# Delta mixer: query, key and head norms kept as token columns, gates first, output slots begun chunk by chunk

## The chip, the cores and the metric

The kernel runs on one core of one Trainium2 chip. The metric is the device time of one execution in microseconds (us); less is better. The core has a matrix engine (PE, its weight loads shown as PEld), a vector engine (DVE), an activation engine (ACT), a general engine (POOL) and a queue engine (SP) that issues loads. PE writes into eight banks of PSUM (128 partitions x 512 fp32 each); DVE and ACT read PSUM, POOL works on SBUF alone. Engines run on their own and wait for one another by semaphores.

## The reference

The program is a two-layer block (adaptive norms, SwiGLU halves, a gated-delta mixer in layer 0 and a window attention in layer 1) followed by a second two-layer block. The change touches the gated-delta mixer and, in one loop order, the three other output projections. Of the mixer this is computed, for 512 tokens (256 context, 256 latent), 8 heads of 128, in both directions:

```python
def _l2_normalize(x):
    return (xf * lax.rsqrt(jnp.sum(xf * xf, axis=-1, keepdims=True) + EPS))
...
qkv, z, ab = jnp.split(h @ w_in, [qkv_w, qkv_w + z_w], axis=-1)
qkv = jax.nn.silu(_short_conv(qkv, conv_w))
g = -jnp.exp(a_log) * jax.nn.softplus(ab[:, :, :, 0] + dt_bias)
beta = jax.nn.sigmoid(ab[:, :, :, 1])
return _l2_normalize(q), _l2_normalize(k), v, z, g, beta
...
# chunkwise gated delta rule in both directions, o_t = S_t^T q_t / sqrt(dk)
...
y = _rms_norm(o_f + o_b, o_gain) * jax.nn.silu(z)
return y.reshape(y.shape[0], y.shape[1], -1) @ w_out
```

So there are three norms over a head's 128 features: of each query, of each key, and of each head's output.

## The kernel before, in words

Activations are kept feature-major: a chunk is 128 features x 512 tokens. Every fp32 weight product is made from two parts, so `product` (lines 618 to 622) issues three matmuls: high x high, low of one x high, high x low. A weight slot (up to 128 x 2048) is loaded by SP into a ring of four; `high` on ACT (line 1287) rounds it into `w_hi`, which has two buffers, and POOL (line 2418, four instructions of 128x512) leaves the low part in `ring_lo`. PE then runs the slot. `slots_used` counts slots that PE is through with, and starts the next `high`.

**The input projection** (`delta_in`). `dn_in` has 16 slots of 48 matmuls, 128x512 each; the first runs chunk by chunk of the activations as the norm before it delivers them. DVE takes the two banks of each of slots 0 to 11 through a 5-tap convolution (lines 2208 and 2212) and a gate with ACT's tanh (lines 1620 and 2221); slots 12 to 15 are the z gate (lines 2230 and 2234). `pr_free` counts banks that are free again. Then comes the slot `dn_ab` (96 matmuls that write 32 columns each: the gates' inputs). Only then ACT squares the 16 query and key chunks (line 1631), PE sums over the 128 features by a matmul with ones, whose result stands in every partition (line 772), ACT takes the root (line 1666), and DVE takes a reciprocal of 128x512 and multiplies (`heads_norm`, lines 2269 and 2271). The decay gates follow, a matmul with a triangle (line 777), and the core.

**The core** (`delta_core`) has 8 units U, each for 4 heads and one 128-token chunk in both directions s. In a unit, six levels n of a triangular inversion alternate PE (lines 842, 854, 857) and DVE (lines 2320, 2328); work of the next unit is put between the levels: decay rows at n = 1 (line 793), the values turned to token-major at n = 2 (line 803, copied by ACT at line 1697), key products at n = 4 (line 809). DVE adds the outputs of both directions into `h` (line 2338).

**The output.** After the last unit `heads_norm` does the same for the 8 output heads (squares, ones matmul at line 943, root, reciprocal, gain, product with z at line 2277). ACT and POOL prepare the weights of `dn_out` after that; DVE splits `h` into high and low (lines 1805 and 1807); PE runs 4 slots of 48 matmuls, bank by bank, and DVE adds each to `x` (line 1861). `project_out` is also used for `swa_out`, `mla_out0` and `mla_out1`.

The order on each engine is the order in which the code is written.

## Time and profile before

| | |
|---|---|
| median of 3 runs | 3388.6 us (3388.38 to 3397.56) |
| the profiled execution's own time | 3385.27 us |
| its span | 3383.4 us |
| PE busy | 3099.0 us (92%), 23172 matmuls |
| DVE / ACT / POOL busy | 43% / 34% / 46% |
| chain that ended last, by engine | PE 56%; POOL 19%; issue 15%; DVE 7%; ACT 2% |

The span is the first to the last instruction; the execution's own time is 1.9 us longer. A busy PE means that a matmul is in flight, not that PE is at its peak. PEclk is the clock that PE was granted, as a share of 2.4 GHz: 1.00 is 2.4 GHz, 0.50 is 1.2 GHz, and a stretch between has parts at both. In a timeline row the bracket tells how long the engine sat idle before the row and which instruction ended that; where there is no bracket the idle time was under about 0.15 us. "x48 3.07" rows are merged: so many instructions that follow one another, and the time from the first's start to the last's end.

### The profile page before, as it was taken

The page shows a single profiled execution, that of the slowest core. Times are in us where ns is not written, and L with a number is a line of the kernel's source. Part 1 is how long each engine was busy: PE and PEld are TensorE (multiplying, and loading weights), DVE is VectorE, ACT ScalarE, POOL GpSimd, SP SyncE. Part 2 cuts the span into 40 slices and gives each one's busy share as a digit, 9 for nine tenths or more (in the row PEclk, how much of TensorE's full clock was granted, in tenths as well). Part 3 has the DMA queues.
Part 4 walks back from the last instruction along what each step waited for, and adds up shares of the span by engine and source line. Part 5 has one row for each costly group of instructions (what it writes and reads, how often), then busy time and mean ns, then how long its engine had stood idle before and what let it go on. Part 6 is the DMA issues. An engine that isn't in the chain of part 4 may idle for free.

```text
span 3383.4 us, 56078 instructions
## 1 busy us (share of the span) xinstructions
PE 3099.0 (92%) x23172; PEld 2684.4 (79%) x23172; DVE 1454.7 (43%) x2565; ACT 1136.2 (34%) x1720; POOL 1540.5 (46%) x1183
## 2 busy tenths in 40 slices
PE   6999999949998489999899997989999899998998
PEld 4777778828887367777778877789987899887998
DVE  3222348585555732123321245542454452355452
ACT  2212223232222122121322224543354464454563
POOL 1444434301010334444344543179881588662686
PEclk8999989969999789999899998999999899999899
DMA  7534322200000133443433232045542355441454
GB/s 289 170 122 163 124 92 99 76 13 3 2 3 2 36 138 123 165 162 110 149 127 126 82 114 75 27 137 188 186 151 84 112 186 174 137 150 63 141 173 133
DMA packets 58915, 390.04 MB, mean 115 GB/s; under 512 B 6480, under 2 KB 7760, under 8 KB 21360
## 3 DMA queue, kind: packets, MB, share of 16 engines
q1 hardware_dynamic: 49472, 322.07, 27.7%
q10 hardware_dynamic: 9072, 64.25, 5.5%
q8 instruction: 132, 2.16, 0.3%
q0 software_dynamic: 192, 1.18, 0.1%
q14 instruction: 47, 0.39, 0.0%
HBM read 386.42 MB, written 1.05 MB: 115 GB/s over the span
## 4 chain that ended last, share of the span: by engine, by line
PE 56%; POOL 19%; issue 15%; DVE 7%; ACT 2%; DMA 0%; POOLq 0%; ACTq 0%; DVEq 0%
POOL ring_lo L2418 19%; PE bank L620 14%; PE bank L621 13%; PE bank L622 13%; DVE core L2269 2%; PE bank L655 1%; PE bank L1130 1%; PE bank L854 1%; PE bank L842 1%; PE bank L857 1%; DVE core L2328 1%; PE bank L1035 1%; PE bank L1141 1%; PE bank L793 1%; PE bank L1023 1%
## 5 line engine op out<-in xcount | busy, mean ns | idle before, releaser
L2418 POOL TENSOR_TENSOR ring_lo<-ring,w_hi 128x512 fp32r<-128x512 f32 (+1 forms) x833 | 1098.2, 1349 | 1301.6 <-ACT w_hi L1287 1301.3
L622 PE MATMUL bank<-h_hi,ring_lo 128*128 128x256 f32 (+1 forms) x3376 | 1117.8, 331 | 0.0
L620 PE MATMUL bank<-h_hi,w_hi 128*128 128x512 f32 (+1 forms) x2448 | 868.7, 355 | 100.1 <-POOL ring_lo L2418 70.6
L621 PE MATMUL bank<-h_lo,w_hi 128*128 128x512 f32 (+1 forms) x2448 | 854.3, 349 | 0.0
L622 PEld LDWEIGHTS bank<-h_hi,ring_lo 128*128 128x128 f32 x3376 | 654.3, 194 | 58.7
L620 PEld LDWEIGHTS bank<-h_hi,w_hi 128*128 128x128 f32 x2448 | 473.7, 194 | 181.3 <-POOL ring_lo L2418 65.0
L1287 ACT ACTIVATE w_hi<-ring 128x2048 fp32r<-128x2048 f32 (+2 forms) x227 | 395.6, 1743 | 439.9 <-PE bank L622 332.9
L621 PEld LDWEIGHTS bank<-h_lo,w_hi 128*128 128x128 f32 x2448 | 474.2, 194 | 53.6
L622 PE MATMUL bank<-hid_r,ring_lo 128*128 128x256 f32 (+1 forms) x1088 | 364.3, 335 | 0.0
L1877 DVE SCALAR_TENSOR_TENSOR core<-core,bank 128x512 f32<-128x512 f32 (+1 forms) x88 | 54.7, 621 | 641.8 <-ACT core L1355 641.8
L620 PE MATMUL bank<-hid_r,w_hi 128*128 128x512 f32 (+1 forms) x808 | 289.8, 359 | 2.3 <-POOL ring_lo L2418 2.3
L621 PE MATMUL bank<-hid_r,w_hi 128*128 128x512 f32 (+1 forms) x808 | 285.4, 353 | 0.0
L2418 POOL TENSOR_TENSOR ring_lo<-ring,h_hi 128x512 fp32r<-128x512 f32 (+2 forms) x156 | 199.0, 1305 | 103.4 <-ACT h_hi L1287 103.3
L622 PEld LDWEIGHTS bank<-hid_r,ring_lo 128*128 128x128 f32 x1088 | 206.6, 190 | 21.7
L2418 POOL TENSOR_TENSOR ring_lo<-ring,x_r 128x512 fp32r<-128x512 f32 (+2 forms) x156 | 199.9, 1312 | 43.5 <-ACT x_r L1287 43.3
L1355 ACT ACTIVATE core<-bank 128x512 f32<-128x512 f32 (+1 forms) x88 | 47.9, 545 | 492.8 <-PE bank L622 492.8
L1861 DVE SCALAR_TENSOR_TENSOR x<-bank,hgate,x 128x256 f32<-128x256 f32 x112 | 49.8, 480 | 323.1 <-PE bank L622 323.1
L2434 POOL TENSOR_TENSOR core<-core,con 128x512 f32<-128x512 f32 x16 | 20.3, 1287 | 347.0 <-DVE core L2304 347.0
L620 PEld LDWEIGHTS bank<-hid_r,w_hi 128*128 128x128 f32 x808 | 152.9, 189 | 30.9 <-issue 8.2
L621 PEld LDWEIGHTS bank<-hid_r,w_hi 128*128 128x128 f32 x808 | 153.0, 189 | 19.6
L620 PE MATMUL bank<-h_hi 128*128 128x256 f32 x464 | 136.3, 294 | 11.5 <-POOL ring_lo L2418 4.8
L620 PE MATMUL bank<-h_hi,x_r 128*128 128x256 f32 x464 | 131.9, 284 | 3.2 <-POOL ring_lo L2418 1.9
(373 smaller groups left out, 4737.5 us busy)
## 6 DMA issues: line engine op xcount, KB each, us to landing
ring<-w SPq DMA_DIRECT2D x88, 1024.0 KB, 4.9
zbuf<-ada_later ACTq DMA_DIRECT2D x60, 1024.0 KB, 4.9
ring<-up SPq DMA_DIRECT2D x48, 1024.0 KB, 4.8
ring<-w SPq DMA_DIRECT2D x64, 704.0 KB, 4.0
...
```

Source lines behind the costliest of these rows:

```text
L620: pe.matmul(out, a[0], b[0], start=start, stop=False)
L621: pe.matmul(out, a[0], b[1], start=False, stop=False)
L622: return pe.matmul(out, a[1], b[0], start=False, stop=stop)
L655: mm = pe.matmul(out[32 * j:32 * j + 32, :], cond[:, c, :], w[:, c * 256:(c + 1) * 256], start=(c < 4), stop=(c >= 4))
L793: mm = pe.matmul(dbank[s][A0][:, hd, :], dcol(TOK_G, U, s, hd).broadcast_to([P, P]), incl(s), start=True, stop=True)
L842: mm = pe.matmul(small4(s, C0)[r, hd, :], q[f"LT{U % 2}"][r, hd, r], identc[r, :] if n == 0 else q["X"][r, hd, :], start=True, stop=True)
L1287: ins = act.activation(part, like(ring[:, r, a:b], part), ACT.Copy)
L1355: act.activation(tanh2[:, u % 2, t0:T], psum[u % 2][:, t0:T], ACT.Tanh, scale=0.5).then_inc(tanh_done, 1)
L1861: ins = dve.scalar_tensor_tensor(xs, psum[OUT_BANK + c % 2][:, s * CTX:(s + 1) * CTX], gate[:, 2 * c + s:2 * c + s + 1], xs, ALU.mult, ALU ...
L1877: turn(dve.scalar_tensor_tensor(swu2[:, u % 2, t0:T], tanh2[:, u % 2, t0:T], 1.0, psum[u % 2][:, t0:T], ALU.add, ALU.mult))
L2269: step(dve.reciprocal(grec[:, c % 4, :], dstd[:, c % 8, :]))
L2418: ins = pool.tensor_tensor(like(ring_lo[:, r, a:b], part), like(ring[:, r, a:b], part), part.bitcast(F32), ALU.subtract)
```

## The change

The three norms are no longer applied to 128x512 tiles; the sums are formed as columns with one value per token, and the factors are moved to where a per-token factor is applied anyway. Queries and keys stay unnormalised in `qkv`. The key's inverse norm squared goes into beta (`norm_columns`), and the inverse norm itself into the copy of the values (`key_norm_col`). The query's norm scales only the output head, so it cancels in the head's norm but for the epsilon, which gets the query's sum (`query_eps`). The head's norm is summed per unit, and its root and reciprocal are taken once as 128x32; PE spreads the result over partitions by a matmul with the identity.

`dn_ab` is loaded and multiplied before the other slots of `dn_in` (within its first), with the 32 gate columns as stationary side and 512 tokens moving; four small matmuls turn it. The gates are made between slots 1 and 7. Squares and sums of queries and keys follow the slots one by one. The product with z moves to POOL, inside the core. In `project_out` the first slot of the four output projections runs chunk by chunk over both banks. `dn_in` is a plain unrolled loop on PE, ACT and DVE. Line numbers of the changed kernel differ: lines 620 to 622 before are 637 to 639 after.

```diff
-        STREAMS += [("dn_in", 16, 2048), ("dn_ab", 1, 256), ("dn_out", 4, 2048)]
+        STREAMS += [("dn_ab", 1, 256), ("dn_in", 16, 2048), ("dn_out", 4, 2048)]
...
-                    for q in range(2 if parts == 1 else 1):
+                    qs = range(2 if parts == 1 else 1)
+                    first = parts == 1 and n == 0
...
+                wab = weights(pe, "dn_ab", 0, 0)
+                for n in range(16):
...
+                        if n == 0 and q == 0:
+                            ab = product(psum[MISC][0:32, :], cut(wab, lambda v: v(c * 32, (c + 1) * 32)),
+                                         cut(hs, lambda v: v[:, c, :]), c == 0, c == DC - 1)
+                            if c == DC - 1:
+                                ab.then_inc(slots_used, 1)
...
-                over_slots(pe, 16, slot)
-
-                w = weights(pe, "dn_ab", 0, 0)
-                for tc in range(4):
-                    for c in range(DC):
-                        mm = product(psum[MISC][:, tc * 32:(tc + 1) * 32], cut(hs, lambda v: v[:, c, tc * CK:(tc + 1) * CK]),
-                                     cut(w, lambda v: v(c * 32, (c + 1) * 32)), c == 0, c == DC - 1)
-                mm.then_inc(slots_used, 1)
-
-                for c in range(16):
-                    pe.wait_ge(hs_done, c + 1)
-                    if c >= 2:
-                        pe.wait_ge(hstd_done, c - 1)
-                    pe.matmul(psum[4 + c % 2][:, :], ones, sqh[:, c % 4, :], start=True, stop=True).then_inc(hsum_done, 1)
-
-                pe.wait_ge(gates_done, 1)
-                pe.wait_ge(consts_in, 32)
-                for s in range(2):
-                    mm = pe.matmul(psum[MISC][:, 32 * s:32 * (s + 1)], incl(s), tokv(TOK_G)[:, 32 * s:32 * (s + 1)],
-                                   start=True, stop=True)
-                mm.then_inc(gate_pe, 1)
+                    if n == 1:
+                        pe.wait_ge(gate_act, 1)
+                        for tc in range(4):
+                            mm = pe.matmul(psum[STAT][:, 32 * tc:32 * tc + 32], ab_t[:, tc * P:(tc + 1) * P], ident[0:32, 0:32],
+                                           start=True, stop=True)
+                        mm.then_inc(gate_pe, 1)
+                    if 2 <= n < 10:
+                        for c in (2 * n - 4, 2 * n - 3):
+                            pe.wait_ge(hs_done, c + 1)
+                            for tc in range(4):
+                                j = 32 * (c // DNH) + tc * DNH + c % DNH
+                                mm = pe.matmul(psum[OUT_BANK][:, j:j + 1], sqh[:, c % 4, tc * P:(tc + 1) * P], ones[:, 0:1],
+                                               start=True, stop=True)
+                            mm.then_inc(hsum_done, 1)
+                    if n == 6:
+                        pe.wait_ge(gates_done, 1)
+                        pe.wait_ge(consts_in, 32)
+                        for s in range(2):
+                            mm = pe.matmul(psum[STAT][:, 128 + 32 * s:160 + 32 * s], incl(s), tokv(TOK_G)[:, 32 * s:32 * (s + 1)],
+                                           start=True, stop=True)
+                        mm.then_inc(gate_pe, 1)
...
+                def head_sums(U, s):
+                    pe.wait_ge(hs_done, 16 + U - 1 + s + 1)
+                    if U + 2 < UNITS_D:
+                        pe.wait_ge(dn["v"][s], U + 3)
+                    else:
+                        pe.wait_ge(dn["qd"][s], UNITS_D)
+                    for hd in range(QUAD):
+                        mm = pe.matmul(dwide[s][A1][:, hd:hd + 1], quad[s]["LT1"][:, hd, :], ones[:, 0:1], start=True, stop=True)
+                    mm.then_inc(hsum_done, 1)
...
+                            elif n == 3 and U % 2 == 0 and U > 0:
+                                head_sums(U - 1, s)
...
             def delta_out(k):
-                for c in range(DNH):
-                    pe.wait_ge(hs_done, 16 + c + 1)
-                    if c >= 2:
-                        pe.wait_ge(hstd_done, 16 + c - 1)
-                    pe.matmul(psum[6 + c % 2][:, :], ones, sqh[:, c % 4, :], start=True, stop=True).then_inc(hsum_done, 1)
+                pe.wait_ge(hn_done, 9)
+                for hd in range(DNH):
+                    if hd >= 6:
+                        pe.wait_ge(y_in_done, hd - 5)
+                    for tc in range(4):
+                        mm = pe.matmul(psum[HEAD_BANKS[hd % 6]][:, tc * P:(tc + 1) * P],
+                                       head_r[:, tc * DNH + hd:tc * DNH + hd + 1].broadcast_to([P, P]), ident, start=True, stop=True)
+                    mm.then_inc(hd_spread, 1)
                 project_out("dn_out", X_BEFORE[1], hs, DC, 1, 0, ready="dn_out")
...
-                high("dn_in", 1, 0, 1)
-                stream("dn_in", "dn_ab", proj, ahead=2)
-
-                for c in range(16):
-                    if c >= 4:
-                        act.wait_ge(hsum_done, c - 3)
-                    if c == 0:
-                        act.wait_ge(pr_free, 4 + 32)
...
+                high("dn_in", 1, 0, 1, free=BASE["dn_ab"])
+                for n in range(16):
+                    if n + 2 < 16:
+                        high("dn_in", n + 2, (n + 2) // RING, (n + 2) % RING)
...
+                        act.activation(ab_t, psum[MISC][0:32, :], ACT.Copy).then_inc(gate_act, 1)
+                    proj(n, n // RING, n % RING)
+                    if 1 <= n < 9:
+                        for c in (2 * n - 2, 2 * n - 1):
+                            act.wait_ge(pr_free, 4 + c + 1)
+                            if c >= 4:
+                                act.wait_ge(hsum_done, c - 3)
+                            act.activation(sqh[:, c % 4, :], qkv[:, c, :], ACT.Square).then_inc(hs_done, 1)
...
+                    if n == 10:
+                        act.wait_ge(hsum_done, 16)
+                        act.activation(tokv(TOK_T2)[:, 0:32], psum[OUT_BANK][:, 32:64], ACT.Sqrt, bias=eps).then_inc(hstd_done, 1)
...
+                for s in range(2):
+                    head_squares(UNITS_D - 1, s)
+                high("dn_out", 0, 0, 0)
+                act.wait_ge(hn_done, 8)
+                act.activation(head_r, head_r, ACT.Sqrt).then_inc(hstd_done, 1)
                 act_steps[0] = mine.n
-                act.wait_ge(y_in_done, DNH)
-                high("dn_out", 0, 0, 0)
+                for hd in range(DNH):
+                    act.wait_ge(y_in_done, hd + 1)
+                    act.activation(h_hi[:, hd, :], h[:, hd, :], ACT.Copy).then_inc(hh_done, 1)
                 stream("dn_out", "w1_010")
...
+            def head_squares(U, s):
+                act.wait_ge(dn["outd"][s], U + 1)
+                act.activation(quad[s]["LT1"], out_block(h, U, s), ACT.Square).then_inc(hs_done, 1)
...
-                    act.activation(quad[s]["V"], dbank[s][A1], ACT.Copy).then_inc(dn["v"][s], 1)
+                    for hd in range(QUAD):
+                        ins = act.activation(quad[s]["V"][:, hd, :], dbank[s][A1][:, hd, :], ACT.Copy, scale=key_norm_col(U, s, hd))
+                    ins.then_inc(dn["v"][s], 1)
...
+                    if k == 1:
+                        high("dn_in", 0, 0, 0)
...
+                def norm_columns():
+                    dve.wait_ge(gate_act, 4)
+                    dve.tensor_copy(tokv(TOK_GC), psum[STAT][:, 128:192])
+                    dve.wait_ge(hstd_done, 1)
+                    step(dve.tensor_scalar(query_eps, psum[OUT_BANK][:, 0:32], EPS, EPS * P, ALU.add, ALU.mult))
+                    r, rr = tokv(TOK_T3)[:, 0:32], tokv(TOK_T3)[:, 32:64]
+                    step(dve.reciprocal(r, tokv(TOK_T2)[:, 0:32]))
+                    step(dve.tensor_tensor(rr, r, r, ALU.mult))
+                    both = tokv(TOK_BETA).rearrange("p (d c) -> p d c", d=2)
+                    step(dve.tensor_tensor(both, both, rr.unsqueeze(1).broadcast_to([P, 2, 32]), ALU.mult))
+                    dve.tensor_scalar(tokv(TOK_NEGB), tokv(TOK_BETA), -1.0, None, ALU.mult).then_inc(gates_done, 1)
+
+                after = {1: gate_inputs, 4: decay_rate, 11: norm_columns}
...
-                heads_norm(16, DNH)
-                for c in range(DC):
-                    dve.wait_ge(y_in_done, c + 1)
-                    split("dn_out", c, h[:, c, :], 0)
+
+                dve.wait_ge(hstd_done, 2)
+                dve.reciprocal(head_r, head_r).then_inc(hn_done, 1)
+
+                def head_scaled(hd):
+                    dve.wait_ge(hd_spread, hd + 1)
+                    dve.scalar_tensor_tensor(h[:, hd, :], h[:, hd, :], p_("dn_gain"), psum[HEAD_BANKS[hd % 6]][:, :], ALU.mult, ALU.mult)\
+                        .then_inc(y_in_done, 1)
+
+                dve.wait_ge(hz_done, 8)
+                head_scaled(0)
+                head_scaled(1)
+                for hd in range(DNH):
+                    dve.wait_ge(hh_done, h_split("dn_out", hd))
+                    dve.tensor_tensor(h_lo[:, hd, :], h[:, hd, :], h_hi[:, hd, :].bitcast(F32), ALU.subtract).then_inc(hl_done, 1)
+                    if hd + 2 < DNH:
+                        head_scaled(hd + 2)
                 add_out("dn_out", k, 1, mod[:, k, 2, :], 0, squared=k + 1)
...
+                def head_mean(U, s):
+                    dve.wait_ge(hsum_done, 16 + U - 1 + s + 1)
+                    dve.scalar_tensor_tensor(head_cols(head_r, U, s), dwide[s][A1][:, 0:QUAD], 1.0 / P, head_cols(query_eps, U, s),
+                                             ALU.mult, ALU.add).then_inc(hn_done, 1)
...
+                def head_gate(U, s):
+                    pool.wait_ge(hs_done, 16 + U - 1 + s + 1)
+                    block = out_block(h, U, s)
+                    pool.tensor_tensor(block, block, out_block(zs, U, s), ALU.mult).then_inc(hz_done, 1)
```

How the instructions stand on PE where the projection ends and the core begins. Before: the last gate-input matmuls (128x32), 16 sums against ones (L772), two triangle matmuls (L777), and the core's first (L793, L803).

```order
L620 MATMUL bank<-w_hi,h_hi 128x32
L621 MATMUL bank<-ring_lo,h_hi 128x32
L622 MATMUL bank<-w_hi,h_lo 128x32
L772 MATMUL bank<-core,con 128x512 x16
L777 MATMUL bank<-tok,con 128x32 x2
L793 MATMUL bank<-con,tok 128x128 x8
L803 MATMUL bank<-con,big 128x128 x8
```

After: the last matmuls of slot 15 (L637 to L639) are followed by the core's first (L817 is L793 of before, L827 is L803).

```order
L637 MATMUL bank<-h_hi,w_hi 128x512
L638 MATMUL bank<-h_lo,w_hi 128x512
L639 MATMUL bank<-h_hi,ring_lo 128x512
L817 MATMUL bank<-con,tok 128x128 x8
L827 MATMUL bank<-con,big 128x128 x8
```

The 96 gate matmuls, the 16 sums and the 2 triangle matmuls no longer stand between slot 15 and the core. What takes their place stands between slots; this is PE at the end of slot 6 after the change (L794: one-column sums, L801: the triangle):

```order
L638 MATMUL bank<-h_lo,w_hi 128x512
L639 MATMUL bank<-h_hi,ring_lo 128x512
L794 MATMUL bank<-con,core 128x1 x8
L801 MATMUL bank<-tok,con 128x32 x2
L637 MATMUL bank<-h_hi,w_hi 128x512
```

Such eight one-column matmuls stand behind each of slots 2 to 9; before, two slots followed each other directly there.

DVE after the core's last outputs. Before, for each head a reciprocal, the gain and the product with z, and at the end the splits (L1805 and L1807, here the first two of the heads' last rows and the first of the splits):

```order
L2338 TENSOR_TENSOR h<-h,bank 128x4x128 x2
L2269 RECIPROCAL core<-core 128x512
L2274 SCALAR_TENSOR_TENSOR h<-h,par,core 128x512
L2277 TENSOR_TENSOR h<-h,zbuf 128x512
L2269 RECIPROCAL core<-core 128x512
```

After (L2404 is L2338 of before, L2364 the head means, L2327 gain and norm, L2335 the low part):

```order
L2404 TENSOR_TENSOR h<-h,bank 128x4x128 x2
L2364 SCALAR_TENSOR_TENSOR tok<-bank,tok 128x4 x2
L2323 RECIPROCAL tok<-tok 128x32
L2327 SCALAR_TENSOR_TENSOR h<-h,par,bank 128x512 x2
L2335 TENSOR_TENSOR h_lo<-h,h_hi 128x512
L2327 SCALAR_TENSOR_TENSOR h<-h,par,bank 128x512
```

Eight wide reciprocals became one of 32 columns, the product with z is gone from DVE, and the high parts are now ACT's.

## Rows read from the trace of the kernel before

**Rows 1.** Busy time by stretch, all engines; its columns are in its second line

```profile
core 0: us, PE busy (x) PEld busy (x) DVE busy (x) ACT busy (x) POOL busy (x), PEclk, DMA share, GB/s
600.00:660.00 60.00, 60.00 (x268) 49.71 (x266) 33.66 (x43) 14.56 (x16) 24.48 (x19) 1.00 0.21 72
660.00:677.00 17.00, 16.82 (x96) 16.72 (x95) 2.72 (x5) 1.31 (x3) 0.00 (x0) 0.61 0.19 63
677.00:746.60 69.60, 22.92 (x36) 6.88 (x36) 65.01 (x42) 25.34 (x41) 0.00 (x0) 0.62 0.04 15
746.60:1091.00 344.40, 312.65 (x6016) 295.60 (x6016) 183.92 (x442) 82.89 (x232) 35.53 (x28) 0.99 0.01 2
1091.00:1140.00 49.00, 8.65 (x16) 2.46 (x16) 45.04 (x33) 14.42 (x19) 5.37 (x4) 0.63 0.00 1
```

**Rows 2.** Instruction groups 677 to 745 us, DVE: busy us, mean ns, idle before

```profile
L2269 DVE RECIPROCAL core<-core 128x512 f32<-128x512 f32 x16 | 53.5, 3346 | 2.4 <-ACT core L1666 2.4
L2271 DVE SCALAR_TENSOR_TENSOR big<-big,core 128x512 f32<-128x512 f32 x16 | 11.1, 692 | 0.5
```

**Rows 3.** Timeline of PE: start us, us, instruction, idle before and what ended it

```profile
469.68 1.95 PE L639 MATMUL bank<-con,core 128*128 128x1 f32 x16 [1.70 <-DVE core L1817]
472.26 1.87 PE L647 MATMUL bank<-con,tok 128*128 128x128 f32 x8 [0.64 <-DVE tok L1828]
477.11 0.77 PE L620 MATMUL bank<-h_hi,w_hi 128*128 128x512 f32 x1 [2.97 <-DVE h_lo L1842]
482.78 0.40 PE L621 MATMUL bank<-h_lo,w_hi 128*128 128x512 f32 x1
493.59 0.79 PE L620 MATMUL bank<-h_hi,w_hi 128*128 128x512 f32 x1 [2.67 <-POOL ring_lo L2418]
```

**Rows 4.** Timeline of DVE and ACT, slots 1, 11 and 15 of dn_in

```profile
507.94 0.75 DVE L2208 TENSOR_SCALAR core<-bank,par 128x512 f32<-128x512 f32 x1 [6.25 <-PE bank L622]
616.74 0.75 DVE L2208 TENSOR_SCALAR core<-bank,par 128x512 f32<-128x512 f32 x1 [0.39 <-PE bank L622]
625.76 0.64 ACT L1620 ACTIVATE core<-core 128x512 f32<-128x512 f32 x1 [4.01 <-DVE core L2212]
...
660.02 1.29 DVE L2230 TENSOR_SCALAR core<-bank 128x512 f32<-128x512 f32 x2 [8.20 <-PE bank L622]
661.41 1.29 DVE L2234 SCALAR_TENSOR_TENSOR zbuf<-core 128x512 f32<-128x512 f32 x2
```

**Rows 5.** Chain that ended last, from 746 us: start us, us, what

```profile
746.65 3.75 PE bank L793 x16
```

**Rows 6.** Timeline inside one unit of the core

```profile
858.86 0.60 ACT L1697 ACTIVATE core<-bank 128x512 f32<-128x512 f32 x1 [0.30 <-PE bank L803]
862.15 0.63 PE L854 MATMUL bank<-core 64*64 64x64 f32 x16
```

**Rows 7.** Timeline from the core's last output to the second slot of dn_out

```profile
1090.35 0.69 DVE L2338 TENSOR_TENSOR h<-h,bank 128x512 f32<-128x512 f32 x1 [1.10 <-PE bank L893]
1092.30 1.28 ACT L1666 ACT_TABLE_LOAD   x1
...
1132.64 3.71 ACT L1287 ACTIVATE w_hi<-ring 128x2048 fp32r<-128x2048 f32 x2 [30.00 <-DVE h L2277]
1134.63 11.95 POOL L2418 TENSOR_TENSOR ring_lo<-ring,w_hi 128x512 fp32r<-128x512 f32 x8 [77.42 <-ACT w_hi L1287]
1136.21 1.63 DVE L1807 TENSOR_TENSOR h_lo<-h,h_hi 128x512 fp32r<-128x512 f32 x1
...
1147.49 0.69 DVE L1807 TENSOR_TENSOR h_lo<-h,h_hi 128x512 fp32r<-128x512 f32 x1
1155.74 0.88 DVE L1861 SCALAR_TENSOR_TENSOR x<-bank,mod,x 128x256 f32<-128x256 f32 x2 [6.49 <-PE bank L622]
1156.77 0.47 PE L620 MATMUL bank<-h_hi,w_hi 128*128 128x512 f32 x1 [1.06 <-DVE x L1861]
```

**Rows 8.** Timeline of PE, first slot of mla_out1

```profile
3118.59 0.38 PE L620 MATMUL bank<-h_hi,w_hi 128*128 128x256 f32 x1 [2.55 <-DVE h_lo L1807]
```

172 lines of the change are left out of this document (85 added, 87 removed).

## The prediction

> **What bounds the kernel now.** I read first the page's head (PE busy 92%), then busy time by stretch [rows 1], then the groups and timelines of the places that the change touches, PE's first. [Rows 1] name the bound of each stretch. From 600 to 660 us PE is busy all the time at clock 1.00: here matmul time counts. From 660 to 677 us PE does only the 96 gate-input matmuls, at clock 0.61, and DVE has 2.72 us of work. From 677 to 746.6 us DVE is busy 65.01 of 69.6 us and PE 22.9: DVE's reciprocals bound. From 746.6 to 1091 us, the core, PE is busy 312.65 of 344.4 us. From 1091 to 1140 us DVE is busy 45.04 of 49 us, PE 8.65. So the edits at the two stretches that DVE bounds can give time back, and edits in the two that PE bounds cost what they put on PE. The sum is made against the profiled execution's own time, 3385.3 us; it lies 3.3 us below the median of 3388.6, which is added back at the end. A measurement of this kernel can tell 0.3%, 10 us, from no change.
>
> **1. The start of dn_in.** Slot 0 is 48 matmuls. The first 13 take 477.11 to 482.78, 0.436 each; then the clock is up. When they are done PE waits 2.67 us for `ring_lo` (POOL), and slot 1 begins cold, 0.79 for its first matmul, as slot 0's was 0.77 [rows 3]. DVE takes a slot once both its banks are done: slot 1 at 507.94 and slot 15 at 660.02, 14 slots later [rows 4], so a warm slot lasts 10.863 us and a matmul 0.2263. Afterwards slot 0 has 72 matmuls, 24 of them for the gates: 482.78 + 59 x 0.2263 = 496.1. POOL is ready by then (at 493.59 before), so there is neither the wait nor a second cold start, and slot 1 ends at 496.1 + 10.9 = 507.0; with 0.2 for the semaphore DVE has it at 507.2. **Gain: 0.8 us**; the gate matmuls cost nothing, since they take the place of the wait (2.67) and the cold start (13 x 0.21 = 2.7). Were the wait still there, the cost would be 2 us. One change could bring it: the cast of slot 0's weights now waits until PE is through with the last slot of the product before, at 469.68 - 1.70 = 467.98 [rows 3]; the cast takes 1.9 (half of 3.71) and POOL's four pieces 4 x 11.95 / 8 = 6.0 [rows 7], so they end at 475.9, ahead of 477.11 where slot 0 starts.
>
> **2. Between the slots.** The sums of 16 chunks are 64 one-column matmuls. Sixteen of that kind took 1.95 us [rows 3], 0.122 each: 7.8 us. Four transposes and two triangle matmuls add 0.8 (eight 128x128 ones took 1.87 cold): 8.6. Bounds: 5, if they overlap their neighbours, and 15, if each takes the 0.234 of that 128x128 row. ACT's squares (16 x about 0.6, as its 0.64 for a 128x512 tanh) fit in the 4.01 us that it idles in front of a tanh, twice per slot. DVE is near its limit: in a slot of 10.86 us it waits 0.39 us for PE [rows 4]. Its gate work (12 to 14 instructions of 32 to 64 columns, some 3 us in all after slots 1, 4 and 11) goes into that slack, into the 1.0 us by which each slot with sums is longer, and into slots 12 to 15, where it has 2.6 of 10.86 us to do. ACT's table changes (1.28 each [rows 7], four or five) fall in its idle time too. So DVE's start in slot 15 is 660.02 - 0.8 + 8.6 = 667.8. It needs 2.7 us from there for the z gate (660.02 to 661.41 + 1.29), and with 0.1 for the semaphore the core starts at 670.6. Before it started at 746.65 [rows 5]. **Gain: 76.0 us.** What goes is the 17.0 us of gate matmuls and the 69.6 us of norms, in which 16 reciprocals took 53.5 and 16 multiplies 11.1 [rows 2]. What comes last next is the z gate: the core's first matmuls write banks that it reads.
>
> **3. The core.** Sums of a unit's heads stand behind level 3 of units 2, 4 and 6: 8 one-column matmuls, 1.0 us each time, and PE is what the chain goes through there: L854 of the next level would start that much later [rows 6]. **Cost: 3.0 us.** Costed at nothing: the copy of the values in 4 pieces instead of one of 0.60 (L1697; ACT is busy 83 of 344 us, and the values are wanted one unit later), six squares on ACT, six products with z on POOL, which is busy 36 of 344 us [rows 1], and six means of 4 columns on DVE. If ACT's cover is gone, 7 copies cost 1.1 us more each and 6 squares 0.6: that makes 14 the upper end, and 0 the lower (sums in PE's own gaps, of which it has 32 us).
>
> **4. From the core to dn_out.** Call T the end of the last output, 1090.35 + 0.69 = 1091.04 [rows 7]. After T: square 0.6 and a semaphore, 0.7; ACT casts slot 0's weights, 1.9 (3.71 for two), to 2.6; table load 1.28, to 3.9; a root of 32 columns 0.25 (my estimate, under the 0.64 of 512 columns [rows 4]), a reciprocal of 32 columns 0.21 (a sixteenth of 3.346 [rows 2]), and semaphores: the spreads start at T + 4.7. They are 32 matmuls of 128 columns: at 0.234 until the clock is up, then half: 6.8 us, so the first product is at T + 11.5. Slot 0 now runs chunk by chunk, 48 x 0.2263 = 10.9, to T + 22.4. It needs one head per 1.36 us; DVE gives one per 0.7 + 0.69 = 1.4 (the 0.69 is L1807's at 1147.49), and with a start two heads ahead isn't in the way. Slot 1's weights: ACT has the 8 high parts of `h` first, up to T + 17.6, then the cast, to 19.5, then POOL's four pieces at 11.95 / 8 = 1.5, to T + 25.2. So POOL, not PE, sets slot 1's start. Before it was 1156.77 = T + 65.7. That is 40.5 us earlier. The wait of 2.6 us ahead of it is like that of 2.67 in front of 493.59, behind which slot 1 of dn_in started cold; there 13 matmuls at 0.436 instead of 0.2263 cost 2.7. I take off 2.0. **Gain: 38.5 us.** Bounds: 26 (rival C) and 43 (no cold start, ACT's copies beside DVE).
>
> L1807 took 1.63 us at 1136.21, while POOL made low parts, and 0.69 at 1147.49, when it had ended [rows 7]. The Trainium skill, "GPSIMD Engine Reference", section "Key points", says that POOL shares its SBUF interfaces with VectorE and that DVE instructions with two SBUF inputs are among those that suffer. By it the low parts stretch and the scaling, whose second operand is in PSUM, does not. By the row alone all 16 may stretch by 0.94; that is 1.88 per head, rival C's price.
>
> **5. The other output projections.** In mla_out1 PE waits 2.55 us for the last chunk's low part while only its first bank's matmuls are there to do [rows 8]; mla_out0 has the same wait, 2.54, and swa_out has none. With both banks chunk by chunk PE has twice the work per chunk. **Gain: 4.8 us**, between 0 and 5.1.
>
> **Sum**: 76.0 - 3.0 + 38.5 + 4.8 = 116.3, profiled time 3269.0; with 3.3 added the median is 3272.
>
> **Rivals.**
> B, the squares couple the engines: each wait for ACT's squares in 8 slots costs PE another 1.3 us (two squares), 10.4, and the values' and squares' copies in the core take half of its upper end, 14 / 2 = 7 (3 are in the forecast): 3272 + 10.4 + 4 = 3286 to 3288. For it: DVE has only 0.39 us of slack per slot [rows 4], and squares wait for DVE's gate. Against it: sums lag their slot by one, and ACT idles 4.01 us.
> C, the tail is paced by DVE under POOL: POOL works on slots 0 and 1 while DVE scales and splits; with 1.88 more per head it gives the last head at T + 11.5 + 8 x 3.28 = 37.7, and slot 1 follows; 65.7 - 37.7 - 2 = 26 instead of 38.5: 3284. For it 1.63 against 0.69. Against it: slot 0's four POOL pieces end near T + 9, and slot 1's begin after T + 19.
> D, more than forecast: the one-column sums disappear beside their neighbours (up to 7.8 in dn_in, 3 in the core, of which I take two thirds) and dn_out has no second cold start (2): 3272 - 9 = 3263.
> E, slower: the inserted one-column matmuls bring the clock down to 1.2 GHz in slots 2 to 15. Then 14 x 48 matmuls take 0.436 instead of 0.2263: 141 us lost against 116 won, 3413. It decides from 11.5 slots on, 10.1 us each. For it: the stretch of 32-column matmuls had 0.61, busy 16.82 of 17.0 us. Against it: the core, of 6016 short matmuls with gaps, has 0.99 [rows 1].
> The Trainium skill, "TensorE: Matmul & The Clock Gate", section "HAM oscillation — how this bites in real kernels", reports kernels that lose clock to short idle gaps between groups of matmuls; by it alone the time would be E's, by the row of the core, with far more gaps at 0.99, the forecast's.
> F, it doesn't do what it says, and the core still waits for something of the old chain. On PE nothing but slot 15 now stands ahead of the core, and the last gate step on DVE comes after slot 11, so this is all but excluded.
>
> **Chances.** Forecast 0.60 (own range 3262 to 3282), B 0.17, C 0.13, D 0.07, E 0.02, F 0.01. Faster by over 0.3%: 0.97; within: 0.01; slower: 0.02. The range 3260 to 3292 takes in forecast, D, B and C and leaves out the combinations of B and C.
>
> **What would show it.** DVE's start in slot 15 near 667.8 and the core's first matmul near 670.6 (steps 1, 2); a slot with sums at 11.9 us instead of 10.86, at clock 1.00 (else B or E); a core of about 347 us instead of 344.4, with level 4 of units 2, 4 and 6 late by 1 us (step 3); the first product of dn_out at T + 11.5 and slot 1 at T + 25, with a wait for `ring_lo` ahead of it (step 4; with DVE's low parts at 1.6, C); no wait over 1 us for `h_lo` in mla_out0 and mla_out1 (step 5). The forecast is wrong above all if the core's start or dn_out's slot 1 is off by over 5 us.

## The result

| | before | after |
|---|---|---|
| median | 3391.99 us (4 runs, 3388.38 to 3397.56) | 3279.45 us (4 runs, 3276.90 to 3281.89) |
| ratio | | 0.967, 95% interval 0.9653 to 0.9688 |
| profiled execution | 3385.27 us, span 3383.4 | 3281.89 us, span 3280.1 |
| PE busy | 3099.0 us, 23172 rows | 3077.8 us, 23316 rows |

The median was forecast at 3272 and the profiled execution at 3269.0. The medians are 112.5 us apart, the two profiled executions only 103.4: the profiled execution of the kernel before lies 6.7 us below its median, that of the changed one 2.4 above. Single executions scatter more than the steps argued about here: the kernel before took 3382 to 3402 us in all runs of this study, the changed one 3272 to 3290. So the steps are judged by marks inside the profiles, that is, by the times at which named instructions start.

The stretches of the kernel after that answer to [rows 1]: slot 0 to slot 1 of dn_in, slots 1 to 15, the z gate, the core, and from the core to slot 1 of dn_out. The columns are those of [rows 1].

```profile
core 0: us, PE busy (x) PEld busy (x) DVE busy (x) ACT busy (x) POOL busy (x), PEclk, DMA share, GB/s
476.70:506.90 30.20, 30.20 (x121) 22.10 (x121) 19.12 (x39) 12.20 (x18) 10.07 (x8) 0.91 0.20 71
506.90:675.70 168.80, 168.78 (x813) 141.72 (x812) 111.14 (x158) 56.89 (x67) 67.42 (x52) 1.00 0.25 88
675.70:678.60 2.90, 0.05 (x1) 0.08 (x1) 2.72 (x5) 1.23 (x2) 0.00 (x0) 1.00 0.68 192
678.60:1026.70 348.10, 316.69 (x6072) 299.36 (x6072) 184.25 (x448) 94.31 (x287) 44.11 (x35) 1.00 0.01 4
1026.70:1052.50 25.80, 21.44 (x121) 19.05 (x122) 12.02 (x23) 11.74 (x14) 11.46 (x10) 0.87 0.00 1
```

The two stretches that DVE bounded are gone; PE is busy without a gap in all of dn_in. Mark by mark, profile against profile:

| step | forecast gain | measured | from |
|---|---|---|---|
| 1, slot 1 of dn_in | 0.8 | 0.5 | 507.94 to 506.97, less 0.45 by which dn_in began earlier |
| 2, core's start | 76.0 (with step 1) | 67.7 | 746.65 to 678.55, less the same 0.45 |
| 3, core | -3.0 | -3.8 | 344.4 to 348.2 |
| 4, slot 1 of dn_out | 38.5 | 39.9 | 65.7 to 25.8 behind the core |
| 5, mla_out0 and 1 | 4.8 | 5.1 | waits of 2.54 and 2.55 gone |
| not forecast | | 2.3 | dn_in's earlier start 0.45, rest of dn_out 1.1, later 0.8 |
| not forecast | | -1.5 | near 2120 us the clock is at 1.2 GHz for 6.8 us, before for 3.4 |
| not forecast | | -11.5 | one DVE copy of 12.35 us |
| not forecast | | 5.1 | given back in stages behind the copy |
| sum | 116.3 | 103.3 | |

### Slots 1 to 15

DVE's timeline, starts of slots 1, 2, 3 and 15 (answers to [rows 4]):

```profile
506.97 0.75 DVE L2256 TENSOR_SCALAR core<-bank,par 128x512 f32<-128x512 f32 x1 [1.52 <-PE bank L639]
519.08 0.75 DVE L2256 TENSOR_SCALAR core<-bank,par 128x512 f32<-128x512 f32 x1 [1.78 <-PE bank L639]
531.80 0.75 DVE L2256 TENSOR_SCALAR core<-bank,par 128x512 f32<-128x512 f32 x1 [3.43 <-PE bank L639]
...
675.72 1.29 DVE L2278 TENSOR_SCALAR core<-bank 128x512 f32<-128x512 f32 x2 [8.20 <-PE bank L639]
```

Slot 15 was forecast at 667.8. PE's instruction groups between 507 and 672 us say why (columns as in [rows 2]):

```profile
L794 PE MATMUL bank<-con,core 128*128 128x1 f32 x128 | 14.7, 245 | 0.0
L786 PE MATMUL bank<-con,core 32*128 32x32 f32 x8 | 1.1, 274 | 0.0
L801 PE MATMUL bank<-tok,con 128*128 128x32 f32 x4 | 0.6, 276 | 0.0
```

The program has 64 one-column matmuls, and the trace 128 rows of them, 14.7 us instead of 7.8. Transposes and triangle have twice their number too. A slot with sums takes 12.72 us, 1.84 more than one without (10.88), not 1.0. PE waits for nobody in these slots: the squares never come late (rival B), and the clock is 1.00 (rival E). Nor do the sums disappear beside their neighbours (rival D).

### The core

PE in unit 2, around the sums of unit 1's heads (answers to [rows 6]):

```profile
789.85 0.68 PE L878 MATMUL bank<-core 64*64 64x64 f32 x16
790.78 0.68 PE L878 MATMUL bank<-core 64*64 64x64 f32 x16 [0.25 <-DVE core L2394]
791.40 2.11 PE L843 MATMUL bank<-con,core 128*128 128x1 f32 x16
793.44 1.12 PE L890 MATMUL bank<-core 64*64 64x64 f32 x16
```

and granted clock around the same place (PE alone):

```profile
786.00:791.40 5.40, 5.15 (x113) 1.00 0.01 3
791.40:793.40 2.00, 2.00 (x20) 0.91 0.03 8
793.40:796.60 3.20, 3.20 (x63) 0.52 0.00 0
796.60:800.00 3.40, 3.07 (x57) 1.00 0.00 0
```

The sums are 16 rows, 1.95 to 2.1 us, all on the path. Behind them the clock is at 1.2 GHz for 3 us; that adds 1.5 us in unit 2. In units 4 and 6 it stays at 2.4 GHz. From each unit's decay rows to the next ones the loss is 3.5 us in unit 2 and 2.0 in unit 4. From those of unit 6 to the core's end it is 1.0, but here the two kernels do not compare as they stand. The kernel before loses clock 7.5 us before the end of its core, the changed one does not (first row before, second after):

```profile
1083.06 3.41 PE L881 MATMUL bank<-core 128*128 128x128 f32 x16 [1.30 <-ACT core L1711]
1019.78 2.05 PE L917 MATMUL bank<-core 128*128 128x128 f32 x16 [1.30 <-ACT core L1756]
```

From the matmuls ahead of these rows to the core's end the kernel before takes 10.58 us, the changed one 9.55. So the sums of unit 6 cost 2.0 as well, and all sums 7.5. The core wins 2.8 at its start: PE had idled only 2.87 us, and its first decay rows come warm (2.02 us, against 3.75 in [rows 5]). In sum 7.5 - 2.8 - 1.0 = 3.7 of the 3.8 us.

### From the core to dn_out

The core's last output on DVE, ACT, the spreads on PE, POOL's low parts of slot 1 and PE's start in slot 1 (answers to [rows 7]). T is now 1026.73.

```profile
1026.04 0.69 DVE L2404 TENSOR_TENSOR h<-h,bank 128x512 f32<-128x512 f32 x1 [1.10 <-PE bank L929]
1027.30 1.89 ACT L1331 ACTIVATE w_hi<-ring 128x2048 fp32r<-128x2048 f32 x1
1030.50 0.23 ACT L1699 ACTIVATE tok<-tok 128x32 f32<-128x32 f32 x1
1031.17 9.41 PE L985 MATMUL bank<-con,tok 128*128 128x128 f32 x64 [2.68 <-DVE tok L2323]
1040.33 0.48 PE L637 MATMUL bank<-h_hi,w_hi 128*128 128x512 f32 x1
1045.86 5.01 POOL L2487 TENSOR_TENSOR ring_lo<-ring,w_hi 128x512 fp32r<-128x512 f32 x4 [11.67 <-ACT w_hi L1331]
1052.53 0.47 PE L637 MATMUL bank<-h_hi,w_hi 128*128 128x512 f32 x1 [1.06 <-DVE x L1909]
```

The spreads start at T + 4.4 (4.7 forecast), but they are 64 rows, not 32, so the first product is at T + 13.6 instead of 11.5. POOL is done at T + 24.1; slot 1 waits for PE's own slot 0 and for DVE's add, not for `ring_lo`, and starts warm (0.47) at T + 25.8.

### The copy of 12.35 us

The second block's first feed-forward half: DVE, then POOL.

```profile
2218.10 12.35 DVE L1931 CAST hid_r<-core 128x256 f32 x1 [0.17 <-DVE core L1927]
```

```profile
2205.40 10.07 POOL L2487 TENSOR_TENSOR ring_lo<-ring,w_hi 128x512 fp32r<-128x512 f32 x8 [1.40 <-ACT w_hi L1331]
2215.42 5.07 POOL L2487 TENSOR_TENSOR ring_lo<-ring,h_hi 128x512 fp32r<-128x512 f32 x4
2220.45 4.97 POOL L2487 TENSOR_TENSOR ring_lo<-ring,x_r 128x512 fp32r<-128x512 f32 x4
2225.39 4.91 POOL L2487 TENSOR_TENSOR ring_lo<-ring,w_hi 128x512 fp32r<-128x512 f32 x4
```

The same instruction took 1.27 us in the kernel before. Here it ends at 2230.45, when POOL's unbroken row of 20 instructions ends at 2230.30. In the profiles where the copy was not held the row went on for 28 instructions and more, so what ended it here may be the held copy itself. PE waits for what follows the copy:

```profile
PE bank L637 <- DVE hid_r L1932: 8.8, 1, 8.8
```

(us in all, times, longest). Up to 1910 us the lead over the kernel before is 105.95 us; just ahead of this place it is 104.65, behind it 93.1, and at the end 103.3. Of the 10.2 that come back 5.1 are step 5.

### The profile page after: what moved, and what is told of

Its sections match the earlier page's. It is cut to its first block, busy times and chain, and to the rows that moved or that the text cites. A ratio compares the mean times of both kernels' runs of the same rounds, so it can differ in the third digit from the quotient of the medians.

```text
span 3280.1 us, 56094 instructions
## 1 busy us (share of the span) xinstructions
PE 3077.8 (94%) x23316; PEld 2683.6 (82%) x23316; DVE 1353.9 (41%) x2522; ACT 1131.0 (34%) x1753; POOL 1545.2 (47%) x1191
## 4 chain that ended last, share of the span: by engine, by line
PE 62%; POOL 18%; issue 13%; DVE 4%; ACT 2%; DMA 0%; POOLq 0%; ACTq 0%; DVEq 0%
POOL ring_lo L2487 18%; PE bank L637 15%; PE bank L638 15%; PE bank L639 15%; PE bank L672 2%; PE bank L1174 1%; PE bank L890 1%; PE bank L893 1%; PE bank L878 1%; DVE core L2394 1%; PE bank L1079 1%; PE bank L1185 1%; PE bank L699 1%; PE bank L1067 1%; PE bank L817 0%
## 5 line engine op out<-in xcount | busy, mean ns | idle before, releaser
L639 PE MATMUL bank<-h_hi,ring_lo 128*128 128x256 f32 (+1 forms) x3384 | 1118.9, 331 | 0.0
L637 PE MATMUL bank<-h_hi,w_hi 128*128 128x512 f32 (+1 forms) x2448 | 864.9, 353 | 52.0 <-POOL ring_lo L2487 29.0
L639 PEld LDWEIGHTS bank<-h_hi,ring_lo 128*128 128x128 f32 x3384 | 653.4, 193 | 59.6 <-issue 0.5
L637 PEld LDWEIGHTS bank<-h_hi,w_hi 128*128 128x128 f32 x2448 | 470.1, 192 | 130.8 <-issue 50.6
L639 PE MATMUL bank<-hid_r,ring_lo 128*128 128x256 f32 (+1 forms) x1088 | 364.3, 335 | 0.0
L637 PE MATMUL bank<-hid_r,w_hi 128*128 128x512 f32 (+1 forms) x808 | 289.9, 359 | 2.3 <-POOL ring_lo L2487 2.3
L639 PEld LDWEIGHTS bank<-hid_r,ring_lo 128*128 128x128 f32 x1088 | 206.6, 190 | 21.7
L2487 POOL TENSOR_TENSOR ring_lo<-ring,x_r 128x512 fp32r<-128x512 f32 (+2 forms) x156 | 199.1, 1306 | 46.5 <-ACT x_r L1331 46.3
L637 PEld LDWEIGHTS bank<-hid_r,w_hi 128*128 128x128 f32 x808 | 152.9, 189 | 30.9 <-issue 8.2
L637 PE MATMUL bank<-h_hi 128*128 128x256 f32 x464 | 138.0, 297 | 17.9 <-DVE hid_r L1932 8.8
L638 PE MATMUL bank<-h_lo,h_hi 128*128 128x256 f32 x464 | 135.4, 292 | 0.0
L637 PE MATMUL bank<-h_hi,x_r 128*128 128x256 f32 x464 | 132.0, 284 | 3.2 <-POOL ring_lo L2487 2.0
```

The costliest lines, as they stand in the source:

```text
L637: pe.matmul(out, a[0], b[0], start=start, stop=False)
L638: pe.matmul(out, a[0], b[1], start=False, stop=False)
L639: return pe.matmul(out, a[1], b[0], start=False, stop=stop)
L2487: ins = pool.tensor_tensor(like(ring_lo[:, r, a:b], part), like(ring[:, r, a:b], part), part.bitcast(F32), ALU.subtract)
```

## The experiments

Marks are compared within one profile: from slot 0 of dn_in to the core's first matmul (201.9 us in the changed kernel), the core's length (348.2) and from its end to slot 1 of dn_out (25.8).

**The changed kernel again.** No edit.

> The changed kernel once more, unedited. In its first profile one DVE copy (L1931, median 0.43 us) took 12.35 us beside an unbroken row of POOL's low parts, PE idled 8.8 us for it, and of the lead over the kernel before (105.9 us up to there) some 8 us were gone at the end. Theory P: this is an accident of one execution, from how DVE's and POOL's instructions happen to fall against each other; then no copy over 2 us stands at this place in a new profile, and the span is 3272 us, 8 shorter than 3280. Theory Q: the change has shifted the two engines so that it happens in every execution; then a copy of about 12 us is there again and the span is 3280. The marks ahead of that place (slot 15 on DVE at 675.7, core at 678.6, slot 1 of dn_out at 1052.5) are the same within 0.5 us by either.

3281.55 us (3271.76 to 3288.51). No copy over 1.46 us, yet the span is 3285.5 instead of P's 3272. 5.2 us were lost ahead of dn_in (slot 0 at 481.87 instead of 476.66), in the first 45 us; that explains less than half. P holds for the copy alone. Between 2200 and 2250 us this execution wins 11.7 us on that with the copy, and by the end it has lost 10.8 of them again: from slot 0 to the end the two take 2803.6 and 2803.4 us. The other marks do not repeat within 0.5 us either: the core took 350.5 us instead of 348.2. Behind unit 2's sums the clock did not fall (44.8 us instead of 46.3), but it did at the core's start, behind unit 6's sums, and near its end, where no sums stand:

```profile
683.38 2.52 PE L817 MATMUL bank<-con,tok 128*128 128x128 f32 x16 [2.87 <-DVE zbuf L2282]
1025.92 3.68 PE L917 MATMUL bank<-core 128*128 128x128 f32 x16 [1.30 <-ACT core L1756]
```

**One-pass sums.**

```diff
-    mm = pe.matmul(psum[OUT_BANK][:, j:j + 1], sqh[:, c % 4, tc * P:(tc + 1) * P], ones[:, 0:1],
+    mm = pe.matmul(psum[OUT_BANK][:, 2*j:2*j + 2], sq_r[:, c % 4, tc * P:(tc + 1) * P], ones_r[:, :],
```

> The 64 sums of queries and keys between the slots take fp32r operands (ACT rounds the squares), two columns wide instead of one; nothing else. The prediction counted 64 matmuls of 0.122 us, 7.8 us in all; the profile after has 128 rows of one column, 16 per slot, and 1.84 us per slot, 14.7 in all. Theory P: an fp32 matmul is two passes on PE and each is a row of the trace, so the sum miscounted by a factor of two; with one pass the slot period falls from 12.72 to 11.8 us, DVE's start in slot 15 from 675.7 to 668.4, and the time by 7.4 us. Theory Q: the cost lies in switching to a new stationary tile and back, not in passes; then the slot period stays at 12.7 and nothing is gained.

3272.66 us. PE behind slot 2, and DVE's start in slots 3 and 4:

```profile
535.56 0.95 PE L796 MATMUL bank<-ones_r,sq_r 128*128 128x2 f32 x8
```

```profile
535.76 0.75 DVE L2259 TENSOR_SCALAR core<-bank,par 128x512 f32<-128x512 f32 x1 [2.54 <-PE bank L641]
547.59 0.75 DVE L2259 TENSOR_SCALAR core<-bank,par 128x512 f32<-128x512 f32 x1 [2.54 <-PE bank L641]
```

8 rows instead of 16, a slot of 11.83 us, and from slot 0 to the core 194.4 instead of 201.9 us, 7.5 less. P holds. Slot 15 itself is at 673.43, since this execution too began 5.2 us late. The unedited kernel, measured beside it, took 3281.55 us; the single times of the two overlap, so the marks carry this and not the medians.

**Sums twice.**

```diff
+    for again in range(2):
         mm = pe.matmul(psum[OUT_BANK][:, j:j + 1], sqh[...], ones[:, 0:1], start=True, stop=True)
```

> Each of the 64 one-column sums between the slots is issued twice in a row (fp32, as in the changed kernel). Theory P, each costs what it shows on PE (0.23 us for both rows): a slot with sums takes 12.72 + 1.84 = 14.6 us and the core starts 14.7 us later, at 693.3. Theory Q, part of the 1.84 us is a cost of the first one of a group (the wait for its weights and for the squares): a slot takes under 14 us. The clock in slots 2 to 9 stays at 1.00 by both; if the one-column matmuls bring it down, as they seem to do in unit 2 of the core (0.52 for 3 us behind 16 such rows), the slots are longer than 14.6.

3301.89 us. Busy time of PE and granted clock, one row per slot, from DVE's start in slot 3 to that in slot 9:

```profile
538.00:552.50 14.50, 14.50 (x82) 1.00 0.21 73
552.50:568.70 16.20, 16.20 (x83) 0.89 0.18 66
568.70:583.10 14.40, 14.40 (x81) 1.00 0.21 74
583.10:599.70 16.60, 16.60 (x87) 0.90 0.18 63
599.70:615.80 16.10, 16.10 (x82) 0.89 0.19 66
615.80:633.50 17.70, 17.70 (x82) 0.81 0.17 60
```

Where the clock stays at 2.4 GHz a slot takes 14.5 us, as P has it. In five of the eight slots with sums it falls for a while and the slot takes 1.6 to 3.2 us more, with PE busy all the time, so no idle gap brought it down; DVE's start in slot 15, taken from slot 1, is 23.9 us later instead of 14.7. Rival E's mechanism exists, then, at twice the dose. With 1.84 us of one-column matmuls per slot no profile shows it between slots. In the core the link is looser. In each of the eight profiles with sums behind level 3 the clock falls behind at least one of the three groups (unit 2's in six, unit 6's in one, those of units 4 and 6 in one), and in none of the six other profiles does it fall at these places. But it also falls near the core's end in five profiles, the kernel before among them, where no sums stand.

**No copy.**

```diff
-    turn.last(dve.tensor_copy(one(hid_hi), hid2[:, u % 2, t0:T]))
+    turn.last(dve.tensor_tensor(one(hid_hi), hid2[:, u % 2, t0:T], hid2[:, u % 2, t0:T], ALU.max))
```

> In all feed-forward halves DVE's copy of the hidden chunk into its high part (L1931) is a maximum of the chunk with itself (two SBUF operands, same result) in place of a copy. Theory P: only the copy form can be held back for a whole row of POOL instructions; then no instruction of this line takes over 2 us and the lead of 105.9 us at the second block's start is kept: span about 3272. Each takes longer than a copy (0.43 to 1.6 us for 512 columns instead of 0.43), but DVE is idle three quarters of the feed-forward halves, so nothing else moves. Theory Q: any DVE instruction can be held back so; then a long one is found in this profile as well.

3276.94 us, span of the profile 3273.2, the line's longest instruction 1.71 us (median 0.69 instead of 0.43). It fits P, but does not show it: the unedited kernel measured beside it had no long copy in its profile either, and one of the four runs took 3293.86 us. Up to 2200 us this profile runs within 0.5 us of the changed kernel's with its copy; it ends 6.9 us earlier. In this pair, then, some 7 of the 11.5 us that the copy costs on the spot are left at the end, and in the pair of the changed kernel and its repetition next to nothing.

**First slots bank by bank.**

```diff
-    first = parts == 1 and n == 0
+    first = False
```

> The changed kernel with the first slot of the four output projections bank by bank again, as before the change. Theory P: the two waits of 2.5 us for the last low part come back in the first slots of mla_out0 and mla_out1, 5 us in all, and dn_out loses nothing, since the spreads keep PE until 13.7 us after the core's end and the last low part is there at 18.0, before the 22nd of the 24 matmuls of the first bank: slot 1 of dn_out starts 25.8 us after the core's end as now. Theory Q: dn_out needs the new order too; then its slot 1 starts 2 to 5 us later, and the sum is 7 to 10 us.

3289.22 us. PE's waits from 2350 us on, and its start in slot 1 of dn_out (the core ends at 1030.01):

```profile
PE bank L637 <- DVE h_lo L1855: 5.1, 2, 2.5
```

```profile
1055.78 0.47 PE L637 MATMUL bank<-h_hi,w_hi 128*128 128x512 f32 x1 [1.06 <-DVE x L1909]
```

As P has it, both waits are back, and dn_out's slot 1 starts 25.8 us behind the core in either order. In dn_out the chunk-by-chunk order is worth nothing, since the spreads hide what it would.

**Heads' sums in PE's gaps.**

```diff
-    for s in range(2):
-        seen_rows(U, n, s)
+    seen_rows(U, n, 0)
+    if n in (1, 2) and U % 2 == 0 and U > 0:
+        head_sums(U - 1, n - 1)
+    seen_rows(U, n, 1)
```

> In the core the sums of a unit's heads (16 rows of one column, 1.95 us, behind level 3 of units 2, 4 and 6) are cut in two groups of 8, each placed where PE waits 0.95 us for DVE between the two directions, at levels 1 and 2 of the same unit; means and the turn of the values follow. Theory P: the groups of 0.95 us fill these waits, the three units fall back to the periods of the kernel before (unit 2 from 46.3 to 44.6 us between its decay rows and the next ones, unit 4 from 44.8 to 42.8), and the core is 5.5 us shorter, 342.7 instead of 348.2 us. Theory Q: a matmul that DVE's result releases is late by the new group's queue, since PE's wait and the group do not overlap; then the core stays at 348.

3277.52 us (3264.57 to 3286.02). The core, all of it:

```profile
681.50:1022.80 341.30, 314.92 (x6072) 297.95 (x6072) 184.28 (x448) 94.51 (x287) 44.17 (x35) 1.00 0.01 4
```

The means on DVE move along, and the turn of the values waits for them. 341.3 instead of 348.2 us with the same rows: 6.9 won, more than P's 5.5, since unit 2 falls back to 42.8 us as in the kernel before and not to 44.6. With the warm start's 2.8 and the end's 1.0 us step 3 is accounted for: 344.4 - 2.8 - 1.0 = 340.6 is the core without any cost of sums, and in the gaps they cost 0.7. The profile has a copy of 12.35 us at the same instruction as the changed kernel's.

**The old output norm.** The norm of the output heads as in the kernel before, with its ones matmuls and roots:

```diff
-    dve.reciprocal(head_r, head_r).then_inc(hn_done, 1)
-    ... h[:, hd, :], p_("dn_gain"), psum[HEAD_BANKS[hd % 6]][:, :] ...
+    step(dve.reciprocal(grec[:, c % 4, :], dstd[:, c % 8, :]))
+    ... h[:, c, :], p_("dn_gain"), grec[:, c % 4, :] ...
+    dve.tensor_tensor(h[:, c, :], h[:, c, :], zs[:, c, :], ALU.mult).then_inc(y_in_done, 1)
```

> The changed kernel with the output heads' norm as before the change: squares, ones matmuls, roots, eight reciprocals of 128x512 and the product with z on DVE after the core; no sums, means or products of heads in the core. (The epsilon's query factor is left out.) High parts on ACT and the chunk-by-chunk first slot of dn_out stay. Theory P: DVE's eight times 3.35 + 0.69 + 0.69 us and the weights that come only after them set slot 1 of dn_out; DVE is done 42 us after the core's end, the weights 7 later, slot 0 ends near 60 and slot 1 starts 61 us after the core's end instead of 25.8: the time rises by 35, less 6.6 that the core gets back, some 29 us. Theory Q: half of the 40 us came from taking slot 0 chunk by chunk and from ACT's high parts; then slot 1 starts before 50.

3325.47 us (3312.87 to 3329.42). The core has no sums at all and is 342.9 us long, 2.3 above the 340.6 just worked out, because the clock falls near its end here too. It ends at 1021.81; that place, and PE's first products of slots 0 and 1:

```profile
1012.59 3.78 PE L915 MATMUL bank<-core 128*128 128x128 f32 x16 [1.30 <-ACT core L1755]
...
1071.75 0.79 PE L637 MATMUL bank<-h_hi,w_hi 128*128 128x512 f32 x1 [39.06 <-POOL ring_lo L2473]
...
1086.30 0.47 PE L637 MATMUL bank<-h_hi,w_hi 128*128 128x512 f32 x1 [1.06 <-DVE x L1905]
```

Slot 1 starts 64.5 us behind the core (P: 61), 1.2 less than in the kernel before. So nearly all of step 4's 40 us is the norm's, and the order of the first slot and ACT's high parts add 1.2 without it.

**The kernel before, without its 16 reciprocals.**

```diff
-    step(dve.reciprocal(grec[:, c % 4, :], dstd[:, c % 8, :]))
-    ... P ** -0.5 if c < DNH else 1.0, grec[:, c % 4, :],
+    ... 1e-6, dstd[:, c % 8, :],
```

> The kernel before the change, without the 16 reciprocals of 128x512 in the norms of queries and keys (the multiplies take the root times 1e-6 instead; the rest stands). Theory P: the reciprocals (53.5 us) bound the stretch of 69.6 us between the gate inputs and the core, and what comes next is PE's sums and ACT's squares and roots: 22.9 us on PE, 25.3 on ACT; the stretch falls to 30 us and the time by 40. Theory Q: something else in the chain, DVE's multiplies and the gates behind them, holds it above 45 us, and the change's 68 us gain at the core's start came more from the order than from the reciprocals.

3346.09 us against 3386.80 of the kernel before, measured beside it. PE between the gate inputs and the core:

```profile
676.19 0.38 PE L622 MATMUL bank<-w_hi,h_lo 128*128 128x32 f32 x1
677.35 6.20 PE L772 MATMUL bank<-core,con 128*128 128x512 f32 x8 [0.78 <-ACT core L1631]
...
702.91 1.06 PE L777 MATMUL bank<-tok,con 128*128 128x32 f32 x4 [4.81 <-DVE tok L2252]
704.76 3.75 PE L793 MATMUL bank<-con,tok 128*128 128x128 f32 x16 [0.79 <-issue]
```

28.2 us from the last gate matmul to the core instead of 70, as P has it. The reciprocals alone were worth 42 us there, 40.7 by the medians. DVE's start in slot 15 and the core were 86.6 us apart before and are 2.8 apart after; the other half needed sums and gates to go elsewhere. Its profile has a copy of 12.35 us as well, and it is a kernel without the change.

**Root before cast.**

```diff
-    high("dn_out", 0, 0, 0)
     act.wait_ge(hn_done, 8)
     act.activation(head_r, head_r, ACT.Sqrt).then_inc(hstd_done, 1)
+    high("dn_out", 0, 0, 0)
```

> Behind the core ACT takes the root of the head means first and casts the weights of dn_out's slot 0 after it (the other way round in the changed kernel). Theory P: the cast of 1.89 us stands on the path to the spreads, and neither POOL's low parts (4.9 us, wanted 9.6 us after the root) nor slot 1 become late: the spreads start 2.7 instead of 4.4 us after the core's end, slot 1 of dn_out 24.1 instead of 25.8, a gain of 1.7 us that only the marks can show. Theory Q: slot 1 waits for ring_lo instead, whose chain is ACT's copies of h, cast and POOL; then it stays at 25 or more.

3279.63 us. The core ends at 1029.89; spreads, first product, slot 1:

```profile
1032.56 10.16 PE L985 MATMUL bank<-con,tok 128*128 128x128 f32 x64 [0.91 <-DVE tok L2323]
1042.47 0.48 PE L637 MATMUL bank<-h_hi,w_hi 128*128 128x512 f32 x1
...
1054.67 0.47 PE L637 MATMUL bank<-h_hi,w_hi 128*128 128x512 f32 x1 [1.06 <-DVE x L1909]
```

The spreads start 1.8 us sooner, at 2.7 as P has it, but last 9.9 instead of 9.2 us: behind the earlier start the clock stays at 1.2 GHz longer (until 5.7 us behind the first spread, against 4.2 in the changed kernel). Slot 1 starts at 24.8. Neither theory had that; 1.0 of the 1.7 us is left. The unedited kernel measured beside it (below) took 3285.81 us; a difference of 6 us by medians is scatter more than it is this edit.

**The three together, and the changed kernel beside it.**

> Three edits of the runs before together: one-pass sums between the slots (7.2 us by its marks), the heads' sums in PE's gaps inside the core (6.9 us), root before cast (1.7 us). Theory P: they touch different stretches and add up: core at 668.4 from a start without delay, core 341.3 us long, slot 1 of dn_out 24.1 us behind it, and a median 15.8 us below that of the unedited kernel of this call. Theory Q: less, since slots with sums of 11.8 us leave DVE or ACT behind, or PE's clock falls where the gaps are filled; then one of these marks is missed by over 1 us.

> The changed kernel unedited a third time, for comparison in the same call: core at about 678.6 plus the delay of this execution's first 45 us (0 to 6 us so far), core 346.7 or 348.2 us (with or without a fallen clock behind the sums of unit 2), slot 1 of dn_out 25.8 us behind the core, median 3280 within 4. The copy of 12.35 us was there in 2 of 7 profiles of kernels of this family, so with a chance of 0.3 it is here too.

3273.11 us (3266.39 to 3277.58) against 3285.81 (3284.12 to 3289.67) measured beside it, 12.7 less where 15.8 were expected. By the marks the edits add up: slot 0 to core 194.5 (201.8 unedited), core 341.3 (348.3), core to slot 1 24.9 (25.7), 15.0 in all. Both profiles have the copy of 12.35 us. The unedited kernel's median is 2 us above what was allowed for it: medians scatter from one measurement to the next by more than I took it to be.

**And no copy.**

> The combination before (one-pass sums, heads' sums in PE's gaps, root before cast) and with it the maximum of the chunk with itself in place of DVE's copy into the hidden chunk's high part. The copy of 12.35 us, always the same one (second block's first feed-forward half, 2.2 ms in), stood in 5 of 10 profiles of the kernels that have the change and the copy, so it is in no fixed tie with an edit. Theory P: only the copy form can be held back so: no instruction of this line over 2 us in the profile, and since half of the executions lose some 8 us to it, the median falls from 3273 to about 3269. Theory Q: the hold-up finds another instruction, or costs nothing net; then the median stays at 3273 or above and a DVE row of over 10 us that is no scan stands somewhere.

3263.33 us (3261.18 to 3270.55), ratio to the kernel before 0.9623 (0.9600 to 0.9647); longest instruction of the line 1.71 us. This beats the changed kernel, whose ratios were 0.967 to 0.969. It was not measured beside the combination that keeps the copy (ratio 0.9642, 0.9617 to 0.9666), and the intervals overlap, so the share of the last edit is not shown by times. By marks the two profiles differ by 7.2 us from slot 0 to the end, and all of it arises behind 2200 us.

## Why the prediction was right, and where it was off

The median lies in the range, and the main mechanism of the forecast stands: both stretches that DVE bounded are gone and PE's own work takes their place. Not everything did what it was to do. The prediction named as its sign of being wrong that the core's start or dn_out's slot 1 is off by over 5 us, and the core starts 8 us late (678.55 instead of 670.6). The profiled time is 12.9 us above its forecast; the median is only 7.5 above, because that execution happens to lie 2.4 us above its kernel's median where the forecast took it to lie 3.3 below. Steps 3 and 4 came out near by errors that cancel.

- **Step 1** held: slot 0 without a wait and without a second cold start.
- **Step 2** had one term mis-sized. "64 one-column matmuls, 0.122 each" took a time per row of the trace times a count of instructions of the program. An fp32 matmul is two rows, two passes, as the halved rows of the one-pass sums show. The rows ahead of the prediction held it: the order has L793 as x8 and [rows 5] the same eight as x16. The term is 16.7 us between slots 1 and 15 instead of 8.6; the upper bound of 15 was too low as well. This is the 8 us by which the core starts late.
- **Step 3** came out near by luck. The sums cost 7.5, not 3.0 (the same factor of two makes 6.0, a fallen clock in unit 2 the other 1.5). A warm start of the core gave 2.8 that I had not priced, and 1.0 came from a fallen clock that the kernel before happens to have near its core's end.
- **Step 4** was 1.4 us better than forecast. The spreads were mis-sized by the same factor (9.2 instead of 6.8 us), the last DVE add is a term that I left out (1.06), and the second cold start did not come (2.0). What sets slot 1's start is PE, not POOL as I had it; POOL's chain was forecast for T + 25.2 (19.5 and four pieces of 1.5 make 25.5) and ended at T + 24.1. Rival C did not happen: low parts took 0.69 us, since POOL was idle while DVE made them. In the old-norm kernel, where they met, eight took 13.14 us. The Trainium skill, "GPSIMD Engine Reference", section "Key points", names two SBUF inputs as a case of contention between the two engines; these low parts have two, and 1.64 against 0.69 us agrees.
- **Step 5** held, 5.1 us of waits.
- **Missing** was the loss by one DVE copy, 11.5 us on the spot. It stood in 6 of the 12 profiles of kernels that have that copy, one of them a kernel without the change, always at the same instruction and with 12.33 to 12.35 us. So it belongs to the execution, not to the change; the profile before happened to be without it and the profile after with it. What of it is left at the end is not settled: two pairs of profiles say 7 us, a third next to nothing. It may be most of the 9.1 us between the 103.4 by profiles and the 112.5 by medians, but executions without a profile do not tell whether they had it.

Open stays what decides whether that copy is held back. It started 12.69 to 12.71 us behind the first of POOL's row in the six profiles where it took 12.35 us, and 12.69 to 12.72 behind it where it took 1.27. Open too is what loses 0 to 5.6 us in the first 45 us of an execution, and what brings the clock down inside the core.
